# Eight of twelve lower parts of the second block's input projection: from VectorE to GpSimd

## The reference

```
r = rms(x, norm1)                       # 256 x 1024
z = r @ w_in                            # 1024 x 2572: the input projection
swa q, k, v = z[:, 0:512], z[:, 512:640], z[:, 640:768]
fox q, k, v and gates, mlstm q, k, v and gates = z[:, 768:2572]
q, k = rope(rms(q)), rope(rms(k))       # of the sliding-window attention, by head of 64
```

## Time and profile before

| | us |
|---|---|
| median of 3 runs | 2011.35 (2008.25 to 2012.51) |
| the profiled execution, its time | 2013.33 |
| the profiled execution, its span | 2011.8 |
| TensorE busy in it | 1753.5 (87%) |
| VectorE busy | 774.0 (38%) |
| ScalarE busy | 642.6 (32%) |
| GpSimd busy | 29.5 (1%) |

### The profile page before, as it was taken

One profiled execution on the slowest core, in us unless ns is written; L12 is line 12 of the kernel. 1 busy time (PEld: TensorE's weight loads), 2 busy tenths in 40 slices (PEclk: granted clock), 3 DMA queues, 4 the chain that ended last, 5 costly groups with the idle time before them and its releaser, 6 DMA issues.

```text
span 2011.8 us, 22089 instructions
## 1 busy us (share of the span) xinstructions
PE 1753.5 (87%) x9214; PEld 1288.5 (64%) x9214; DVE 774.0 (38%) x1476; ACT 642.6 (32%) x1041; POOL 29.5 (1%) x49
## 2 busy tenths in 40 slices
PE   6998986899997998986899995857899988588999
PEld 5777985444435777985444434844599977447997
DVE  4445343210115545333210015643455545515554
ACT  3326422010004336422011013443344444415442
POOL 4000000000000000000000000000000000000000
PEclk9998998799998998998899997965899998678999
DMA  8332345499995432335499992510255545003552
GB/s 258 138 126 93 147 147 219 176 401 421 421 420 178 153 125 89 147 147 218 173 414 421 421 421 99 197 40 0 84 189 188 178 142 183 1 21 126 189 189 105
DMA packets 57663, 392.67 MB, mean 195 GB/s; under 512 B 7124, under 2 KB 7168, under 8 KB 15696
## 3 DMA queue, kind: packets, MB, share of 16 engines
q1 hardware_dynamic: 54144, 380.30, 49.4%
q0 software_dynamic: 3264, 9.61, 1.4%
q10 hardware_dynamic: 144, 1.24, 0.2%
HBM read 390.07 MB, written 1.05 MB: 194 GB/s over the span
## 4 chain that ended last, share of the span: by engine, by line
PE 79%; DVE 10%; ACT 5%; DMA 4%; issue 2%; SPq 0%; DVEq 0%; ACTq 0%
PE psum L538 76%; DMA ring_sb<-in_weights 4%; PE psum L664 2%; ACT ring_rounded L1127 1%; DVE ring_rounded L1469 1%; PE psum L583 1%; ACT region_sb L1153 1%; DVE x_sb L1580 0%; ACT xT_hi_rounded L1352 0%; DVE x_sb L1578 0%; DVE region_sb L1853 0%; DVE region_sb L1856 0%; DVE small_sb L1849 0%; ACT region_sb L1341 0%; DVE region_sb L1847 0%
## 5 line engine op out<-in xcount | busy, mean ns | idle before, releaser
L538 PE MATMUL psum<-ring_sb,region_sb 128*64 128x512 f32 (+1 forms) x1728 | 427.0, 599 | 14.9 <-ACT region_sb L1341 11.0
L1469 DVE TENSOR_TENSOR ring_rounded<-ring_sb,ring_rounded 128x2048 fp32r<-128x2048 f32 (+4 forms) x152 | 321.5, 2130 | 245.6 <-ACT ring_rounded L1127 245.4
L538 PE MATMUL psum<-xT_hi_rounded,ring_rounded 128*128 128x256 f32 x1920 | 357.9, 288 | 0.0
L1127 ACT ACTIVATE ring_rounded<-ring_sb 128x2048 fp32r<-128x2048 f32 (+4 forms) x152 | 268.1, 1781 | 212.7 <-PE psum L538 149.9
L538 PEld LDWEIGHTS psum<-ring_sb,region_sb 128*64 128x64 f32 (+1 forms) x1728 | 148.2, 144 | 277.5 <-issue 260.1
L538 PE MATMUL psum<-ring_rounded,xT_hi_rounded 128*128 128x384 f32 (+4 forms) x960 | 278.3, 367 | 37.1 <-DVE ring_rounded L1469 18.1
L538 PE MATMUL psum<-xT_lo_rounded,ring_rounded 128*128 128x256 f32 x960 | 285.8, 298 | 27.9 <-DVE ring_rounded L1469 16.8
L538 PEld LDWEIGHTS psum<-xT_hi_rounded,ring_rounded 128*128 128x128 f32 x1920 | 308.3, 197 | 1.8 <-issue 0.5
L538 PEld LDWEIGHTS psum<-ring_rounded,xT_hi_rounded 128*128 128x128 f32 x960 | 184.4, 198 | 61.9 <-issue 39.4
L538 PEld LDWEIGHTS psum<-xT_lo_rounded,ring_rounded 128*128 128x128 f32 x960 | 189.7, 198 | 31.6 <-issue 18.1
L538 PE MATMUL psum<-ring_rounded,region_rounded 128*128 128x512 f32 x768 | 178.7, 392 | 3.0 <-DVE region_rounded L2055 3.0
(11 more groups left out here) (239 smaller groups left out, 1345.1 us busy)
## 6 DMA issues: line engine op xcount, KB each, us to landing
ring_sb<-in_weights SPq DMA_DIRECT2D x324, 1024.0 KB, 7.8
ring_sb<-in_weights SPq DMA_DIRECT2D x24, 768.0 KB, 4.3
ring_sb<-in_weights SPq DMA_DIRECT2D x8, 904.0 KB, 4.5
ring_sb<-in_weights SPq DMA_DIRECT2D x8, 900.0 KB, 4.6
ring_sb<-in_weights SPq DMA_DIRECT2D x8, 584.0 KB, 14.3
region_sb<-in_mem POOLq DMA_DIRECT2D x2, 1024.0 KB, 8.5
region_sb<-in_pool_band POOLq DMA_DIRECT2D x2, 1024.0 KB, 10.0
region_sb<-in_ln_g POOLq DMA_DIRECT2D x4, 512.0 KB, 4.3
```

Of the source, the lines that this page charges most:

```text
L538: return nc.tensor.matmul(dst, lhsT, rhs, start=first, stop=last, skip_group_check=True)
L1127: nc.scalar.activation(rounded(piece.hi), piece.raw, ACT.Copy).then_inc(hi_made, 1)
L1469: nc.vector.tensor_tensor(rounded(piece.raw), piece.raw, reread(piece.hi), ALU.subtract).then_inc(lo_made, 1)
```

## The change

In each layer of the second block the lower parts of pieces 4 to 11 are made by GpSimd, by a new function `gpsimd_second`, in the order of the pieces and with a semaphore of their own, `pool_lo_made`. VectorE's `round_lo` passes over them. Pieces 0 to 3 and all other lower parts stay on VectorE. TensorE waits for the one or the other semaphore. To make room for the new semaphore, the signals of the second block's attention stages share those of the first block, with counts that go on from there; the order of the work in them is the same.

```
-        hi_made, lo_made = sem("weights_hi"), sem("weights_lo")
+        hi_made, lo_made, pool_lo_made = sem("weights_hi"), sem("weights_lo"), sem("weights_lo_pool")
+        first_pieces = 2 * len(Z_CUTS) + 4 + 2 + 18 + 4 + PAIRS * 12
+        second_pieces = 2 * len(Z2_CUTS) + 4 + 4 * D_FF // BANK
+        second_first = [first_layers * first_pieces + l * second_pieces for l in range(second_layers)]
...
             if piece.split:
-                pe.wait_ge(lo_made, piece.split_count)
+                pe.wait_ge(*piece.lower)
...
-        n_split = 0
-        for piece in ring.pieces:
-            n_split += piece.split
-            piece.split_count = n_split
+        n_upper = n_lower = n_pool = 0
+        by_pool = [at + n for at in second_first for n in range(4, 2 * len(Z2_CUTS))]
+        for n, piece in enumerate(ring.pieces):
+            piece.on_pool = n in by_pool
+            n_upper += piece.split
+            n_lower += piece.split and not piece.on_pool
+            n_pool += piece.on_pool
+            piece.split_count = n_upper
+            piece.lower = (pool_lo_made, n_pool) if piece.on_pool else (lo_made, n_lower)
...
-                if piece.split:
+                if piece.split and not piece.on_pool:
                     v.wait_ge(hi_made, piece.split_count)
...
+        def gpsimd_second(l):
+            for n in range(4, 2 * len(Z2_CUTS)):
+                piece = ring.pieces[second_first[l] + n]
+                g.wait_ge(hi_made, piece.split_count)
+                nc.gpsimd.tensor_tensor(rounded(piece.raw), piece.raw, reread(piece.hi), ALU.subtract).then_inc(pool_lo_made, 1)
...
             vector_second(l)
+            gpsimd_second(l)
             sync_weights()
```

More of the change, by code:

```diff
@@ L118, with __init__ @@
 class Signal:
-    def __init__(self, sem, per_layer):
-        self.sem, self.per_layer = sem, per_layer
+    def __init__(self, sem, per_layer, before=0):
+        self.sem, self.per_layer, self.before = sem, per_layer, before
     def at(self, l, i=0):
-        return self.sem, l * self.per_layer + i + 1
+        return self.sem, self.before + l * self.per_layer + i + 1
     def last(self, l):
-        return self.sem, (l + 1) * self.per_layer
+        return self.sem, self.before + (l + 1) * self.per_layer
 class Steps:
@@ L459, in build_program, with signal_after @@
         ring = Ring(slots_of_ring, [sem(f"ring_in{i}") for i in range(RING)], [(packed(piece), split) for piece, split in plan])
-        hi_made, lo_made = sem("weights_hi"), sem("weights_lo")
+        hi_made, lo_made, pool_lo_made = sem("weights_hi"), sem("weights_lo"), sem("weights_lo_pool")
+        first_pieces = 2 * len(Z_CUTS) + 4 + 2 + 18 + 4 + PAIRS * 12
+        second_pieces = 2 * len(Z2_CUTS) + 4 + 4 * D_FF // BANK
+        second_first = [first_layers * first_pieces + l * second_pieces for l in range(second_layers)]
         def signal(name, per_layer):
             return Signal(sem(name), per_layer)
+        def signal_after(first, per_layer):
+            return Signal(first.sem, per_layer, first_layers * first.per_layer)
         x_in, consts_in, params_in, router_in, positions_in, out_stored = (
@@ L481, in build_program @@
         memT_made, mk_made, mv_made, mq_made = (
-            signal(n, c) for n, c in (("memT_made", 4), ("mk_made", 4), ("mv_made", 2), ("mq_made", 4)))
+            signal(n, c) for n, c in (("memT_made", 4), ("mk_made", 4), ("mv_made_sinks_exped", 2), ("mq_made", 4)))
         related, scored = signal("related", 16), signal("scored", 16)
@@ L486, in build_program @@
         dsa_scored, dsa_lowered, dsa_exped, dsa_shared, dsa_turned, dsa_out = (
-            signal(n, c) for n, c in (("dsa_scored", 16), ("dsa_lowered", 2), ("dsa_exped", 16), ("dsa_shared", 2),
-                                      ("dsa_turned", 6), ("dsa_out", 8)))
+            signal(n, c) for n, c in (("scores_masked", 16), ("tops_lowered", 2), ("rows_exped", 16), ("rows_shared", 2),
+                                      ("probs_turned", 6), ("values_out", 8)))
         mem_scored, mem_lowered, mem_exped, mem_shared, mem_turned, mem_out = (
-            signal(n, c) for n, c in (("mem_scored", 8), ("mem_lowered", 2), ("mem_exped", 8), ("mem_shared", 2),
-                                      ("mem_turned", 4), ("mem_out", 8)))
+            signal(n, c) for n, c in (("scores_copied", 8), ("side_tops_lowered", 2), ("side_rows_exped", 8), ("side_rows_shared", 2),
+                                      ("side_probs_turned", 4), ("side_values_out", 8)))
         gate_opened, weighed, merged = signal("gate_opened", 24), signal("weighed", 24), signal("merged", 16)
@@ L506, in build_program @@
         swa_scored, swa_lowered, swa_exped, sink_exped, swa_shared, swa_turned, swa_out = (
-            signal(n, c) for n, c in (("swa_scored", 16), ("swa_lowered", 2), ("swa_exped", 16), ("sink_exped", 2),
-                                      ("swa_shared", 2), ("swa_turned", 6), ("swa_out", 8)))
+            signal_after(n, c) for n, c in ((dsa_scored, 16), (dsa_lowered, 2), (dsa_exped, 16), (mv_made, 2),
+                                            (dsa_shared, 2), (dsa_turned, 6), (dsa_out, 8)))
         sink_lowered = signal("sink_lowered", 2)
@@ L514, in build_program @@
         fox_scored, fox_lowered, fox_exped, fox_shared, fox_turned, fox_out = (
-            signal(n, c) for n, c in (("fox_scored", 8), ("fox_lowered", 2), ("fox_exped", 8), ("fox_shared", 2),
-                                      ("fox_turned", 3), ("fox_out", 4)))
+            signal_after(n, c) for n, c in ((mem_scored, 8), (mem_lowered, 2), (mem_exped, 8), (mem_shared, 2),
+                                            (mem_turned, 3), (mem_out, 4)))
         mls_qk_made, mls_open, mls_gated, mls_lowered, mls_weighed, mls_floored, mls_scored, mls_turned = (
```

## The result

The changed kernel takes 2026.7 us in the median of 4 runs (2026.35 to 2027.21), against 2009.8 us in the median of 4 runs for the kernel before: the ratio is 1.0084, with a 95% interval from 1.0067 to 1.0102. It is slower by about 17 us (13.5 to 20.5 by the interval), where 9.5 were forecast; its value lies inside the stated range and near the third rival's 2029.

A forecast was written before the change was run, and what follows sets the result against it. It took TensorE's 5.96 us wait for `swa_heads` before the transposes, in both passes, as the bound. Block losses of 1.15 + 0.3 + 2 × 4.06 = 9.5 us on 2011.35 gave 2021 us, range 1993 to 2031.

The forecast's parts named there:

- third rival: End of `swa_heads`: both late pieces (9 and 10) get in, 2 × 4.06 us more, 2029 us; chance 0.20.
- What bounds the stage: Second block's input projection: TensorE idles 5.96 us a pass before the query transposes, released by the last line of `swa_heads`.
- The price of a subtraction: GpSimd's time for one lower part, called G: taken as 4.06 us, twice VectorE's 2.03; bounds 2.03 and 6.1.
- G hidden by TensorE's matmuls: Cuts 2 and 3: GpSimd's lower parts come before TensorE wants them, even at 6.1 us each.
- The full block, turns in order of arrival: VectorE beside GpSimd: a two-input VectorE instruction waits for the whole GpSimd one, served in order of arrival.
- The first three blocks: Pieces 6 to 8 against `swa_heads`: 9.2 us lost against 8.05 won, 1.15 later; second pass 0.3 later.
- `swa_heads` may start at 1260.70: Head norms on VectorE, first pass: start at 1260.70 instead of 1268.75, 8.05 us won.
- Rival 1: VectorE and GpSimd don't hinder each other; gap and slow clock go, 16.3 us less, 1995 us; chance 0.25 near 1995.
- The late pair: Pieces 9 and 10 at the end of `swa_heads`: one taken to block, 4.06 us a pass; bounds 0 and 8.1.
- The slow clock: The 4.4 us behind TensorE's gap run at clock 0.50; without the gap, 2.2 us less a pass.
- The sum: Whole kernel: 1.15 + 0.3 + 2 × 4.06 = 9.5 us slower; TensorE's gap near 11 us.

The follow-up runs named there:

- interleaved: Kernel before, orders alone changed: VectorE runs `swa_heads` per token block, lower parts of pieces 7, 8 after each; ScalarE's first two roots precede piece 8's upper part; 1993.5 us.
- apart: Changed kernel, but GpSimd makes only the lower parts of pieces 4, 5 and 11, where VectorE has no work; 6 to 10 back on VectorE; 2012.1 us.
- halves: Changed kernel, but GpSimd makes each lower part in two instructions of half the size; 2029.5 us, ratio 1.0092.
- one_input: Changed kernel, but GpSimd copies the raw piece onto itself, rounded, in place of subtracting (another result); 2017.7 us, one run.
- early_back: Changed kernel, but the lower parts of pieces 6, 7 and 8 go back to VectorE, ahead of the head norms; 2022.6 us, ratio 1.0059.
- none: Changed kernel, but nobody makes the lower parts of pieces 4 to 11; TensorE reads the upper part instead (another result); 2007.0 us, ratio 0.9982.

## Why the prediction was right in kind and short in size

- *What bounds the stage.* Right: the gap ahead of the transposes, ended by the last line of `swa_heads`, in both passes. `interleaved` closes it and gains 18 us in the median of its four runs (15 to 21 by the interval), where 16.3 were worked out for a gap and a slow clock gone.
- *The price of a subtraction.* Taken as 4.06 us; measured 4.08 where nothing ran beside it, and up to 4.57 where GpSimd itself was held. The estimate by the ratio of the Trainium skill, GPSIMD Engine Reference, § 3.1 Elementwise, was 3.98.
- *G hidden by TensorE's matmuls.* Right: no gap of TensorE is ended by GpSimd, and `apart` costs nothing.
- *The full block, turns in order of arrival.* Right, by `halves`, `one_input` and `early_back`.
- *The first three blocks.* The net was near, 0.7 and 0.0 us a pass (8.14 and 7.47 less 7.46) where 1.15 and 0.3 stood. The step "`swa_heads` may start at 1260.70", counted as 8.05 us won, was wrong in what it was worth: the first root stands behind the upper part of piece 8 in ScalarE's list. The gain was 3.5 us. The square's block of 2.4 us then cost nothing, since VectorE would have waited anyway; only L1865's 0.4 and L1868's 3.8 counted. Two errors of some 5 us went against each other, so that this part came out near is luck. Rival 1, 1995 us, had the same flaw: it could not have come about by this change, as `none` shows.
- *The late pair.* This is the term that was mis-sized: "I take one, 4.06 us a pass". Both pieces got in, one before the last add and one before the copies, for 7.46 us. The bound of 8.1 was near and rival 3's account of it, that both get in, was right. Piece 9's upper part was done at about 1284.28; GpSimd started at 1284.36, while L1506 still ran, and L1507 found it there. GpSimd noticed within about 0.1 us, which was "against" this rival.
- *The slow clock.* The prediction added nothing for the longer gap, and that holds: the stretch behind it, 1293.20 to 1296.60, has 0.50, and the matmuls from 1296.60 on 1.00; the slow part is no longer than before.
- *The sum.* The gaps account for 15.6 us of the 17 measured (13.5 to 20.5 by the interval). The two profiled executions differ by only 13.0 us, and against the kernel before in the later runs, 2011.0 to 2011.9 us, it would be 15. These differences are within what the clock of the attention stage moves, and the rest stays open. TensorE's gap was to be near 11 us and was 14.10 and 13.43.

## What to carry to other kernels

A second engine is no free one if it goes to memory by the same way: look at what the first does in the very time into which the work moves, and count a whole instruction of the slower engine for each meeting, however short the instruction that it meets. Not every pair collides: here a sum with one input and, beside a fill, the adds kept their time. Before work is moved off an engine, look whether its place in the order is the trouble; here a new order took nearly all of the 11.9 us of gap away, and the move would have taken 7.0 if nothing had been held. And of a head start, follow the first step that another engine must answer: its list has an order too.

## What the runs showed of the hardware that was not expected

- GpSimd's subtraction of 128 x 1800 takes 4.08 us (two back to back in the second pass, ahead of VectorE's square, 8.15), a copy with rounding 1.70 and a fill 1.60. So the subtraction with its second input takes more than twice the time of a copy, where a copy takes hardly more than a fill.
- The granted clock of the attention stage differs from pass to pass and moves the time by some 3 us with the work unchanged. The chain of the kernel before shows about the same matmuls in both passes:

```profile
1349.79 8.23 PE psum L538 x49
...
1739.12 5.51 PE psum L538 x49
```

  In the changed kernel it is 5.51 us in the first pass and 8.17 in the second, in `halves` 8.20 and 10.72, some 2.6 more than in the changed kernel each time, and in `none` 5.51 and 10.72; the group has 49 or 50 matmuls in the first pass of each and 55 in the second. In the kernel before, TensorE is busy for 2.54 of the 15.0 us ahead of this stretch in the first pass and for 2.29 of 15.0 in the second, at a granted clock of 0.50; in the 13 and 10 us with these matmuls the clock is 0.63 and 0.87. What makes one pass differ from the other is not shown. So differences of some 4 us or less between these kernels should be read from the gaps and not from the time.
